# Two-block transformer kernel: sums of weight blocks (seven half products for eight) in two more products of the second block

## The reference

```python
h = rmsnorm(x, norm_mix_g)
proj = h @ w_in                       # 2048 x 8704: qa ka va qb kb vb (4608 columns), then ga gb
ya = sliding_window_attention(qa, ka, va, sinks) @ w_branch_a
yb = stick_breaking_attention(qb, kb, vb) @ w_branch_b
x = x + (sigmoid(ga) * ya + sigmoid(gb) * yb) @ w_out
gate, up = split(rmsnorm(x, norm_ffn_g) @ w_ffn_in)      # 2048 x 11264
x = x + (silu(gate) * up) @ w_ffn_down                   # 5632 x 2048
return rmsnorm(x, norm_final_g)
```

## Time and profile before

| | |
|---|---|
| runs | 2562.51, 2566.71, 2566.54 us; median 2566.54 |
| profiled execution, its own time | 2565.88 us |
| its span, first to last instruction | 2563.9 us |
| granted TensorE clock, mean | 0.997 |
| PE busy | 2531.6 us, 11440 matmuls |
| DVE busy, ACT busy, POOL busy | 1762.9, 1300.4, 271.8 us |
| moved by DMA | 615.41 MB, 240 GB/s |

### The profile page before, as it was taken

The page is one execution under the profiler, slowest core; times in us unless marked ns, Lnnn a source line. Parts: engine busy times, 40 slices in busy tenths (PEclk is TensorE's granted clock), DMA queues, the critical chain, the costliest instruction groups (busy, mean ns, idle before and its releaser), DMA issues.

```text
span 2563.9 us, 30770 instructions
## 1 busy us (share of the span) xinstructions
PE 2531.6 (99%) x11440; PEld 2059.2 (80%) x11440; DVE 1762.9 (69%) x2002; ACT 1300.4 (51%) x1631; POOL 271.8 (11%) x317
## 2 busy tenths in 40 slices
PE   7999999999999999999999999999999999999998
PEld 3887888878888888888888877888888888888887
DVE  4969889967777776555565678466667777765454
ACT  2453456455555455444544467454555555554443
POOL 0021133100000000000100125001011111100000
PEclk9999999999999999999999999999999999999999
DMA  9979988967888887676677554665789999976664
GB/s 369 412 258 346 309 264 270 346 195 244 280 254 274 261 236 214 190 204 205 189 234 215 180 148 123 190 196 176 227 243 264 280 264 281 266 250 203 193 193 156
DMA packets 384371, 615.41 MB, mean 240 GB/s; under 512 B 121700, under 2 KB 122076, under 8 KB 383740
## 3 DMA queue, kind: packets, MB, share of 16 engines
q1 hardware_dynamic: 345920, 513.87, 62.9%
q0 software_dynamic: 31312, 97.70, 13.0%
q10 hardware_dynamic: 7020, 2.26, 0.6%
HBM read 587.53 MB, written 2.10 MB: 230 GB/s over the span
## 4 chain that ended last, share of the span: by engine, by line
PE 94%; DVE 2%; DMA 2%; ACT 1%; issue 1%; SPq 0%; POOL 0%; ACTq 0%; DVEq 0%
PE gp L1764 24%; PE gp L1766 23%; PE gp L1765 23%; PE gp L2346 5%; PE gp L2348 5%; PE gp L2347 5%; DMA proj<-in_w_ada_dram 1%; DVE w_lo L2366 1%; PE tp L2318 1%; PE tp L2319 1%; PE tp L2317 1%; PE gp L2318 0%; PE gp L2319 0%; PE gp L2317 0%; DMA raw<-in_w_in_dram 0%
## 5 line engine op out<-in xcount | busy, mean ns | idle before, releaser
L2366 DVE TENSOR_TENSOR w_lo<-raw,w_hi 128x1024 fp32r<-128x1024 f32 x700 | 864.0, 1238 | 538.4 <-ACT w_hi L1072 535.8
L1072 ACT CAST w_hi<-raw 128x1024 fp32r<-128x1024 f32 x700 | 731.5, 1049 | 799.4 <-PE gp L1766 662.3
L1764 PE MATMUL gp<-w_hi,h_hi 128*128 128x512 f32 x1932 | 762.7, 395 | 1.2 <-DVE w_lo L2366 1.1
L1766 PE MATMUL gp<-w_hi,h_lo 128*128 128x512 f32 x1932 | 752.5, 389 | 0.0
L1765 PE MATMUL gp<-w_lo,h_hi 128*128 128x512 f32 x1932 | 752.2, 389 | 0.0
L1764 PEld LDWEIGHTS gp<-w_hi,h_hi 128*128 128x128 f32 x1932 | 362.7, 188 | 85.1 <-issue 8.5
L1766 PEld LDWEIGHTS gp<-w_hi,h_lo 128*128 128x128 f32 x1932 | 362.7, 188 | 76.7
L1765 PEld LDWEIGHTS gp<-w_lo,h_hi 128*128 128x128 f32 x1932 | 362.9, 188 | 73.5 <-issue 0.2
L1764 PE MATMUL gp<-w_hi,a_hi 128*128 128x512 f32 x704 | 274.3, 390 | 0.0
L1765 PE MATMUL gp<-w_lo,a_hi 128*128 128x512 f32 x704 | 273.9, 389 | 0.0
L1766 PE MATMUL gp<-w_hi,a_lo 128*128 128x512 f32 x704 | 273.9, 389 | 0.0
(11 more groups left out here) (394 smaller groups left out, 2293.6 us busy)
## 6 DMA issues: line engine op xcount, KB each, us to landing
raw<-in_w_in_dram SPq DMA_DIRECT2D x248, 512.0 KB, 4.5
raw<-in_w_up_dram SPq DMA_DIRECT2D x176, 512.0 KB, 4.6
raw<-in_w_ffn_in_dram SPq DMA_DIRECT2D x167, 512.0 KB, 6.1
ada_ring<-in_w_ada_dram POOLq DMA_DIRECT2D x128, 512.0 KB, 5.7
raw<-in_w_down_dram SPq DMA_DIRECT2D x88, 512.0 KB, 4.2
raw<-in_w_ffn_down_dram SPq DMA_DIRECT2D x88, 512.0 KB, 4.3
proj<-in_w_ada_dram SPq DMA_DIRECT2D x64, 512.0 KB, 8.7
raw<-in_w_out_dram SPq DMA_DIRECT2D x64, 512.0 KB, 5.0
```

The costliest lines, as they stand in the source:

```text
L1072: nc.scalar.copy(w_hi[:, s], raw[:, r]).then_inc(hi_ready, 1)
L1764: mm(o, hi[:, kt0 + kt, ps], w_hi[:, s, k, :], start=n == 0, stop=False)
L1766: return mm(o, lo[:, kt0 + kt, ps], w_hi[:, s, k, :], start=False, stop=n == g.kts - 1)
L2366: V.tensor_tensor(w_lo[:, s], raw[:, g.raw_slot(e, j)], w_hi[:, s].bitcast(F32), ALU.subtract).then_inc(lo_ready, 1)
```

## The change

The class of the seven-product scheme is split in three: `UpGemm` (as before), `InGemm` for `g_in2a` and `DownGemm` for `g_down2`. A unit now carries a set number m.

- `g_in2a`: chunk pairs 1, 2 and 3 (of 4 pairs and a single last chunk) use the same 19-unit order as the up product, one set each. The sums of activations `s_in` are made in pair 0 (DVE steps after units 8, 9, 11 and 14, ACT after 13). The weight sums lie in `gates2`, in the first case where the scratch of these activation sums lay, so POOL waits for the last of the steps (`s_parts` 2) before it opens T1 and T3 of pair 1. The planes of q and k are now copied after unit 5 or 17 of a pair, and turned after the load of unit 10 or 18.
- `g_down2`: pair 0 (table `TWO`) has two sets, 36 whole and 14 half units, pair 1 (table `THREE`) three sets, 32 whole and 21 half units; before, each pair had 44 whole ones. Partial results of all sets of a pair gather in `tp` and are added once per pair (eight DVE additions, `add_down`).
- The stages that read `x_rows`, `h_hi` and `h_lo` keep the activation sums of `g_down2` (`halves_of_rows`, DVE; a cast on ACT).
- The load of the final gain into `gate2` moves behind the last weight sum, and the multiplications by it into the last chunk.
- PE's list for `g_in2a`, a loop before, is written out. Some semaphores are shared by more signals.

```diff
+class InGemm(UpGemm):
+    FIRST, LAST = 1, 3
+class DownGemm(SevenGemm):
+    FIRST, LAST = 0, 1
+    TWO = (whole(0, 4, 5, 6, 7, 8, 9, 10, 11) + (half("T1", 0), half("B11", 0)) + whole(0, 12) + (half("T3", 0),)
+           + whole(0, 13) + (half("B21", 0), half("T2", 0)) + whole(0, 14) + (half("T1", 1),) + whole(0, 15)
...
-    g_in2a = gemm(w_in_2, N_QKV2 // CW)
+    g_in2a = gemm(w_in_2, N_QKV2 // CW, kind=InGemm)
...
-    g_down2 = gemm(w_ffn_down_2, D // CW)
+    g_down2 = gemm(w_ffn_down_2, D // CW, kind=DownGemm)
...
+            def t_open(g, i, m):
+                t_add(g, i, m, 0, 0, "T1", False)
+                t_add(g, i, m, 1, 0, "T3", False)
+                pool.wait_ge(t_landed[2 * m], g.t_count(i, "T1", t_base(g, "T1", m)) - 16)
+                t_add(g, i, m, 1, 0, "T1", True)
+                pool.wait_ge(t_landed[2 * m + 1], g.t_count(i, "T3", t_base(g, "T3", m)) - 16)
+                t_add(g, i, m, 1, 1, "T3", True)
...
+            pool.wait_ge(s_parts, 2)
+            for i in range(g_in2a.FIRST, g_in2a.LAST + 1):
+                if i > g_in2a.FIRST:
+                    pool.wait_ge(lo_ready, g_in2a.find(i - 1, "T4") + 1)
+                t_open(g_in2a, i, 0)
+                t_second(g_in2a, i, 0)
+                t_third(g_in2a, i, 0)
...
+                    if i == 0 and n in (8, 9, 11, 14):
+                        halves_of_a((8, 9, 11, 14).index(n), in_full, in_sums, s_in, 1)
+                    if seven and n in (9, 12, 14, 16):
+                        if n == 9 and i > g_in2a.FIRST:
+                            dve.wait_ge(drained[0], g_in2a.chunk(i - 1, 1) + 1)
+                        add_p(g_in2a, i, {9: 0, 12: 1, 14: 2, 16: 4}[n], in_p1, in_u, in_w)
```

More of the change, by code:

```diff
@@ L104, with sets @@
 class SevenGemm(Gemm):
[L107 to L111, removed]
+    def sets(self, i):
+        return 1
     def __init__(self, *args):
         super().__init__(*args)
-        assert self.nb == 8
-        self.pairs = self.chunks // 2
-        self.plain = tuple(("all", e, j) for e in range(2) for j in range(self.nb))
+        self.pairs = (self.chunks + 1) // 2
+        self.plain = tuple(("all", e, j, 0) for e in range(2) for j in range(self.nb))
         starts = [self.block0]
@@ new lines, in last, with half, whole @@
+    def last(self, i, name):
+        return self.find(i, name, self.sets(i) - 1)
+def half(name, m=0):
+    e, d = {"T1": (0, 0), "B11": (0, 0), "T2": (0, 0), "T3": (0, 0), "T4": (0, 0), "B21": (0, 1), "B22": (1, 1)}[name]
+    return (name, e, 2 * m + d, m)
+def whole(e, *js):
+    return tuple(("all", e, j, 0) for j in js)
+class UpGemm(SevenGemm):
+    FIRST, LAST = 1, 9
+    SEVEN = ((half("T1"),) + whole(0, 2, 3) + (half("B11"),) + whole(0, 4) + (half("T2"),) + whole(0, 5)
+             + (half("T3"),) + whole(0, 6) + (half("B21"),) + whole(0, 7) + (half("T4"),)
+             + whole(1, 2, 3) + (half("B22"),) + whole(1, 4, 5, 6, 7))
@@ L858, in stream_up2, with stream_down2 @@
                 for i in range(g.pairs):
[L859 to L867, removed]
+                    for n in range(len(g.units(i))):
+                        if i or n >= RING:
+                            load_unit(g, i, n)
                         if i and n == (8 if g.seven(i) else 6):
                             turn(i - 1)
[L870 to L874, removed]
+            def stream_down2():
+                g = g_down2
+                for i in range(g.pairs):
+                    for n in range(len(g.units(i))):
+                        load_unit(g, i, n)
+                        if i == 0 and n == 6:
+                            turn(g_up2.pairs - 1)
             for g, nxt in zip(gemms[3:], gemms[4:-1]):
+                if g is g_in2a:
+                    stream_in2a()
+                    continue
                 if g is g_up2:
@@ L1710, in _ @@
                         swiglu_side(i - 1)
-            prime(g_down2)
+            for n in range(RING):
+                split_unit(g_down2, 0, n)
             def x_down2(c_):
@@ new lines, in stream_down2 @@
+                        last.then_inc(block_used, 1)
+                i, us = g.pairs - 1, g.units(g.pairs - 1)
+                alls = [q for q, u in enumerate(us) if u[:2] == ("all", 1)]
+                pe.wait_ge(lo_ready, g.unit(i, alls[-1]) + 1)
+                for t in range(ST):
+                    for n in alls[-2:]:
+                        for k in range(KB):
+                            last = whole_one(i, n, 1, us[n][2], k, t, alls)
+                        if t == 1:
+                            last.then_inc(block_used, 1)
+                    if t == 0:
+                        last.then_inc(first_rows, 1)
@@ L3007, in odd_or_even @@
+            prime(g_in2b, range(RING - 1))
+            drain_in(g_in2a.pairs - 1, 0)
+            prime(g_in2b, (RING - 1,))
             def odd_or_even(k, odd):
```

638 lines of the change are left out of this document (436 added, 202 removed).

## The result

Five runs of the changed kernel took 2577.44 to 2588.67 us, median 2581.43; beside them the kernel before took 2562.51 to 2566.71, median 2566.1. The ratio is 1.0063, with a 95% interval of 1.0052 to 1.0075: the kernel became 15 us slower, where no change was forecast (2566.5 us, range 2558 to 2573). The profiled execution took 2578.39 us, its span is 2576.5. The granted clock of these five executions is 0.994 to 0.995 in the mean, that of the kernel before 0.997 in its profiled one.

The account below looks back on a forecast made before the run. PE was taken as the bound, without slack. -10.9 + 7.2 + 1.7 + 1.8 + 0.2 = 0.0 on the profiled 2565.9 us; the median of runs is 0.7 higher, so 2566.5, range 2558 to 2573.

Parts of the forecast that it names:

- The down product: Step for `g_down2`: weight sums arrive in time, T2 of set 0 in pair 0 tightest; 0.2 us, bounds 0 and 3.
- A wait of PE over 3 us in `g_down2`: One of the signs, stated beforehand, by which the forecast falls.
- The saving: In `g_in2a` and `g_down2`: 48 matmuls fewer at 0.2267 us each, 10.9 us gained.
- The wait for T1: In `g_in2a`, first unit of pair 1: PE waits for the late-opened sum, 7.2 us, range 6.9 to 11.9.
- The clock: Behind the wait for T1 in `g_in2a`: half clock for some 3.4 us, costing 1.7 us, bounds 0 and 3.4.
- The turns at the pairs' ends: In `g_in2a`: next pair's loads queue behind planes and transposes; 1.8 us, largest before the last chunk, dearer end 6.2.
- put down as hidden: In `g_in2a`: DVE's added splits and additions fit, about 34 us of work in a pair taking PE 42.2 us.
- More DMA is no bar.: In the down product: added DMA is harmless, as the up product works at share 0.97 with 0.3 us wait.
- DMA under load: Rival for `g_in2a`: adding loads and loads after turns land late, 4.7 and 4.4 us more, 2575.6 us; chance 0.2.
- Rival 1's easier half: In `g_in2a`: T1 wait of 5.8 us, nothing for clock and turns, 2561.4 us; the whole faster rival's chance 0.25.
- the rivals 1 and 3: T1's wait short or absent, 2555.8 us, chance 0.25; change not doing what it says, 2577.4 us, chance 0.02.

Follow-up runs that it names:

- the kernel with the down product alone and T2 first: The changed kernel with the input product plain and the load for T2 of set 0 ahead of set 1's adding loads; 2560.69 us, ratio 0.9978.
- T2 first: The changed kernel with the down product's load for T2 of set 0 issued before set 1's two adding loads; 2575.09 us, ratio 1.0034.
- T1 opened early: The changed kernel with the input product's activation-sum scratch moved, so POOL opens T1 of pair 1 earlier; median 2580.86 us, ratio 1.007.
- two sets with no urgent opening: The changed kernel with T2 first and input-product sets in pairs 2 and 3 only, pair 1 plain; 2561.38 us, ratio 0.9984.
- the second, at 2581.18 us: A profiled execution from running the changed kernel once more, nothing altered; that series had median 2581.02 us, ratio 1.0058.
- both edits: The changed kernel with T1 of pair 1 opened earlier and T2 of set 0 ahead of set 1's adding loads; 2567.65 us, ratio 1.0011.

## Why the prediction was wrong

The step that failed is "The down product". It took 0.2 us, with bounds 0 and 3, and 10.0 were there: the stage is 3.2 us longer, and without its 30 matmuls it should be 6.8 shorter. A wait of PE over 3 us in `g_down2` was among the prediction's own signs of being wrong, and it came. The steps for `g_in2a` held for the wait of T1 and the clock, with sizes a little small, and in part for the small waits.

- **The saving, 10.9 us.** Right. PE has 11392 matmuls, and where nothing disturbs, as in the kernel with the down product alone and T2 first, 5.9 of 6.8 us come out.
- **The wait for T1, 7.2 us (6.9 to 11.9).** Right in place, cause and range. Between the starts of the two matmuls lie 9.07 us, which is 8.8 more than the pace. DVE's list was followed to within 0.3 us. The plain load took 7.16 us instead of 5.5: the prediction saw that SP may load four blocks more, but counted their end only in favour of the adding load and not their cost to the plain one, beside which they ran. The share of the DMA engines is 0.97 from 1290 to 1304. Opened earlier, the wait goes from the profile, and on top of T2 first 7.7 us go from the median, so the cause is shown.
- **The clock, 1.7 us.** The mechanism held and the size was small: 2.3 us, and it came twice. The Trainium skill (TensorE: Matmul & The Clock Gate, Part 1) has the throttled state as the default; the windows agree, at 0.50 before PE resumes and for about five microseconds of work after it.
- **The turns at the pairs' ends, 1.8 us (0 to 6.2).** What is left of `g_in2a`, 9.9 + 4.1 - 8.8 - 2.3, is 2.9 us. The prediction's lever was the landing of loads, and it was 5.3 us, between the 4.3 and the 6.4 weighed. The size is in the range, the place is not. The largest was to stand before the last chunk; there 0.3 us stand (1437.64), and 1.4 us stand before the fifth unit of pair 2 (1360.5), where a late load meets DVE's additions. Those had been put down as hidden, from DVE's busy time and not from their place in its list. The prediction also took the turn from SP's 2.59 us of issuing; to landing the median is 2.8 before and 4.3 now, 6.1 and 7.1 in the two kernels with T1 opened early. The Trainium skill (DMA: Bandwidth & Descriptors, Issuing engines are not separate DMA queues) has DMAs run on the same 16 DMA engines and interleave, whichever engine started them; the longer turns beside POOL's loads agree with it, at 4.3 us against 2.8.
- **The down product, 0.2 us.** Its times can be put side by side, counted from the start of the stage (2316.5 in the prediction, 2325.9 in after). T1 split: 17.5 forecast, 17.4 measured. T2 needed by PE: 32.6 forecast, and 32.6 by the pace of after (2325.90 + 8 x 2.72 + 10.88 = 2358.54). So DVE's and PE's times were right. T2's load: the prediction lets it start at once and take at most 11.0 us; it started 3.7 us later and took 14.4. That is 7.1 us more, less the 1.7 us of slack 5.4, and PE waited 5.1. Two things were left out. POOL issues in order, and the opening of set 1 stands between T1 and T2 of set 0; that was asked for PE, ACT, DVE and SP, not here for POOL. And the bound of 11.0 came from an opening with two adding loads in flight beside SP's loads, while here three were, T2's the last of them. The experiment that moves one DMA past two others turns 14.4 into 7.2 and takes 7.1 us off the stage. Behind the wait came 2.4 us of half clock. The rest, 10.0 - 5.3 - 2.4 = 2.3, are small waits near 2412 and 2420 at the end of pair 0, where POOL opens the first two sets of pair 1 (loads of `raw` late by up to 5 us at ACT near 2391, 2403 and 2417).
- **"More DMA is no bar."** It was said of the down product and it held there once T2 was first, at a share of 1.00. In `g_in2a` two sets with no urgent opening bring nothing, at 1.02; the difference between the stages isn't settled. The rival "DMA under load" was priced at 2575.6 for this stage, and late loads are real there, but they are not what put the time at 2581: 3.3 us of the error are from `g_in2a` and 9.8 from `g_down2`. The two together, 13.1, less what `g_up2` gave (0.8) and with 0.3 between the first two columns, are the 12.6 us between the spans.
- **Slips of arithmetic.** Rival 1's easier half adds up to 2561.6, not 2561.4, and the shortest wait that the rows give to 5.7, not 5.8. Nothing hangs on either. Of the rivals 1 and 3 nothing came: the wait is 8.8 us, and 48 matmuls are gone.

What stays open is the spread. The first profiled execution of the changed kernel explains 12.6 of the 15.3 us between the medians; the second, at 2581.18 us near the median, explains 15.1 (2579.0 - 2563.9), with both large waits 0.7 or 0.8 us longer and `g_up2` 0.6 us longer. But single executions lie 11 to 16 us above the fastest of the same kernel (2588.67 of after, 2587 with T1 early, 2577.51 with both edits). With T1 early their mean clock is lower by 0.003, which over 2570 us is an estimated 7.7 us lost, so about half of that spread would be more half clock. None of those executions has a profile, and which waits they are isn't shown.

## What to carry to other kernels

A DMA in an engine's list is late by everything that stands ahead of it there, the waits included; when a chain of dependent loads is put into such a list, write down for each link what lies between it and its release, for every chain and not for the most conspicuous one only. Then price a load with what is in flight beside it, not by the median of a quiet stretch. Where one engine is the bound without slack, a scheme that trades its work for transfers has to be tried stage by stage: here it paid in the down product and not in the input product, though the DMA share came near 1.00 in both. And work that is hidden by its sum can still stand in the wrong place, between a late input and the step that needs it.

## What the runs showed of the hardware

- An adding load of 512 KB took 6.1 us with one other adding load beside it for most of its time (T1 of pair 1), 7.2 us issued first of three and 14.4 us issued last of three within 3 us (T2's load in the down product, the same transfer in two orders).
- The DMA transposes of q and k took longer beside weight sums (medians of 14 to landing): 2.8 us before, 4.3 in after, 4.5 with two sets, 6.1 with T1 opened early, 7.1 with both edits.
- A DMA share of 1.00 went with no wait of PE over 42 us in the down product with T2 first (window 2338 to 2380).
- A gap of 2.7 us between the starts of two matmuls was followed by half clock, and the 12 matmuls behind it took 4.3 us against 2.7 (from 1299.88 in the kernel with T1 early); behind one of 2.0 us in the kernel with both edits, at the same place, the clock stayed at 1.00:

```profile
1300.00:1302.00 2.00, 2.00 (x11) 1.65 (x10) 1.22 (x1) 0.06 (x1) 0.00 (x0) 1.00 1.07 286
```
